# The merge's gates move into the SSM stage: one change to a fused mixer kernel on one core

## What is computed

```python
rw, ss, gates = split(h @ w_in)                      # gates: 2 * 1024 columns
ya = rwkv_branch(rw)                                 # 512 x 1024
# SSM branch, tokens in column-major order of a grid 64 wide
z, xbc, dt = split(ss)
xs, bm, cm = split(silu(conv5(xbc)))                 # 32 heads of 64, 4 groups of 8 heads
for each direction (2), group (4), chunk of 128 tokens (2 of context, then 4):
    y_inter = (c @ h) * exp(cum)                     # "old"
    y_intra = sum over the chunk of (c b) seg xdt    # "new", one product per head
    h = h * exp(total) + b^T (decay * xdt)           # "carry"
yb = rms_norm((y + d * xs) * silu(z)) * ssm_norm     # 512 x 2048
ga, gb = split(sigmoid(gates))
out = (ga * (ya @ proj_a) + gb * (yb @ proj_b)) @ w_out
```

## Time and profile before

| | |
|---|---|
| median of 3 runs | 5265.73 us (5258.98 to 5266.15) |
| profiled execution, its own time | 5250.39 us |
| its span, first to last instruction | 5248.6 us |
| SSM stage in it | 1204.7 to 1936.1 us |
| merge stage's gates and branches | 1936.1 to 2218.0 us |

### The profile page before, as it was taken

How to read it: one execution, slowest core, us unless ns; L and a number is a source line. 1 busy time by engine, 2 the same in 40 slices (tenths; PEclk the granted TensorE clock), 3 DMA queues, 4 the chain that set the end, 5 groups by cost and what they waited for, 6 DMA issues and landing times.

```text
span 5248.6 us, 82193 instructions
## 1 busy us (share of the span) xinstructions
PE 4751.9 (91%) x34820; PEld 2970.3 (57%) x34820; DVE 2125.6 (40%) x3933; ACT 1308.2 (25%) x2411; POOL 427.6 (8%) x387
## 2 busy tenths in 40 slices
PE   7889999888988869979997998989998998989999
PEld 4566666676554544454443545554777545544777
DVE  3555555553354551031112345463333245373333
ACT  2333333332222210010001133231222123231222
POOL 0111111100231230000000000010000000020000
PEclk9999999998999979989998999989999999989999
DMA  6100000001001022139996211113221211113221
GB/s 224 73 18 18 18 18 5 5 5 61 24 33 48 17 107 113 72 139 378 410 408 256 74 66 45 47 58 135 96 80 63 78 53 59 43 44 137 97 96 49
DMA packets 72775, 494.75 MB, mean 94 GB/s; under 512 B 9032, under 2 KB 9560, under 8 KB 29784
## 3 DMA queue, kind: packets, MB, share of 16 engines
q1 hardware_dynamic: 72408, 489.49, 24.1%
HBM read 468.47 MB, written 21.00 MB: 93 GB/s over the span
## 4 chain that ended last, share of the span: by engine, by line
PE 77%; DVE 9%; issue 7%; DMA 3%; ACT 2%; POOL 1%; SPq 0%; PEldq 0%; PEld 0%; POOLq 0%; DVEq 0%; ACTq 0%
PE ps L224 74%; PE ps L227 3%; DMA upper<-in_ew 2%; DVE upper L235 2%; DVE upper L243 1%; ACT upper L282 1%; DVE upper L259 1%; DVE lower L235 1%; POOL upper L3349 1%; DVE upper L251 1%; DVE lower L243 1%; ACT lower L282 0%; DVE upper L239 0%; DVE lower L251 0%; DVE lower L239 0%
## 5 line engine op out<-in xcount | busy, mean ns | idle before, releaser
L224 PE MATMUL ps<-lower 128*128 128x512 f32 (+9 forms) x6512 | 1968.3, 464 | 82.4 <-issue 25.1
L224 PEld LDWEIGHTS ps<-lower 128*128 128x128 f32 (+3 forms) x6512 | 993.5, 197 | 772.8 <-issue 596.2
L224 PE MATMUL ps<-upper 64*64 64x64 f32 (+10 forms) x14800 | 916.1, 261 | 144.8 <-DVE upper L251 48.5
L282 ACT ACTIVATE upper<-ps 128x512 f32<-128x512 f32 (+6 forms) x963 | 446.1, 484 | 2006.8 <-PE ps L224 1341.2
L224 PEld LDWEIGHTS ps<-upper 64*64 64x64 f32 (+5 forms) x14800 | 662.2, 147 | 487.7 <-issue 265.5
L224 PE MATMUL ps<-lower,upper 64*64 64x64 f32 (+6 forms) x7216 | 740.1, 320 | 54.3 <-DMA lower<-in_ada 20.0
L224 PE MATMUL ps<-rounded 128*128 128x512 f32 x3072 | 724.5, 398 | 30.7 <-DVE rounded L235 23.2
L224 PEld LDWEIGHTS ps<-rounded 128*128 128x128 f32 x3072 | 586.8, 191 | 167.6 <-ACT rounded L282 26.3
L224 PEld LDWEIGHTS ps<-lower,upper 64*64 64x64 f32 (+3 forms) x7216 | 404.9, 146 | 337.5 <-issue 280.8
L224 PE MATMUL ps<-upper,lower 128*128 128x512 f32 (+4 forms) x1584 | 512.4, 476 | 10.1 <-DVE lower L243 3.2
L282 ACT ACTIVATE upper<-upper 128x128 f32<-128x128 f32 (+11 forms) x619 | 328.3, 536 | 688.2 <-DVE upper L255 167.4
(11 more groups left out here) (81 smaller groups left out, 2189.5 us busy)
## 6 DMA issues: line engine op xcount, KB each, us to landing
lower<-in_ew SPq DMA_DIRECT2D x144, 1024.0 KB, 10.5
upper<-in_ew SPq DMA_DIRECT2D x48, 1024.0 KB, 13.5
lower<-in_b0f SPq DMA_DIRECT2D x16, 2048.0 KB, 7.6
lower<-in_b1f SPq DMA_DIRECT2D x16, 2048.0 KB, 7.5
upper<-in_ada SPq DMA_DIRECT2D x18, 1024.0 KB, 5.8
lower<-in_wrkv SPq DMA_DIRECT2D x8, 1728.0 KB, 7.6
lower<-in_b0g SPq DMA_DIRECT2D x8, 1536.0 KB, 6.3
gad<-upper SPq DMA_DIRECT2D x48, 256.0 KB, 2.0
```

Of the source, the lines that this page charges most:

```text
L224: return self.e.matmul(out, lhsT, rhs, start=start, stop=stop)
L282: self.e.activation(out, in_, func, bias=bias, scale=scale, accum_out=accum).then_inc(line.up(*event), 1)
```

## The change

The gates' 128 matmuls leave the merge stage. The projector makes them as `mgate`, t, s after its last z: 16 tiles t of four steps with two matmuls each, from column-major `b.hp`. ScalarE copies each tile out of PSUM in row-major order into one of two stages, SP stores it to a new DRAM tensor `gmd`, and the merge stage fetches it into the buffers of the sigmoid, which works in place. The weights come in tiles of 512 columns through the SSM stage's ring. The copies back to `k.hL` and the "scan" meeting go. A group is ready for the scans before its z; the projector may begin group g - 2's successor when both scans of g - 2 are through, and from its second tile on when `gated` says that z of g - 2 is used up. In `apply` each head's product is made as two, one for each half of the stationary matrix's columns (64 each), which write the two halves of the PSUM partitions. The loads of `wdt` and the first `wx` are issued by SP from the RWKV stage's list. Left out of the diff below: new scratch and line declarations, and dispatch lines.

```diff
@@ -129,7 +129,7 @@
     o["wdt"] = tiles(w[:, s + 5120:s + 5184], 64)
     g = s + 5184
     ga, gb = (w[:, g + 1024 * i:g + 1024 * i + 1024].reshape(1024, 8, 128) for i in range(2))
-    o["wg"] = tiles(np.concatenate([ga, gb], 2).reshape(1024, 2048), 256)
+    o["wg"] = tiles(np.concatenate([ga, gb], 2).reshape(1024, 2048), 512)
     o["pa"] = tiles(a["proj_a"][0], 128)
     o["pb"] = tiles(a["proj_b"][0], 128)
     o["wo"] = tiles(a["w_out"][0], 256)
...
@@ -827,6 +828,9 @@
     for name, j, *at in b.order:
         if name == "lora" and at == [1, 1] and j < 6:
             ring.load(("wrkv", j + 2), T["wrkv"][j + 2], P.pe, "lora", j + 2, 1, 1)
+        elif name == "lora" and at == [1, 1] and j == 7:
+            sp.wait_ge(P.pe, "lora", 7, 1, 1)
+            ssm_begin(k, sp)
         elif name == "ada_row" and j < 11:
             modulation(j + 1)
         elif name == "store":
@@ -1486,6 +1490,7 @@
     b.ysum = [m(512) for _ in range(2)]
     b.ysq, b.yd = m(512), m(512)
     b.yo = [m(512) for _ in range(2)]
+    b.stage = [m(512) for _ in range(2)]
     b.xd, b.xe = ([extra(512) for _ in range(2)] for _ in range(2))
     b.cbm = [extra(128) for _ in range(2)]
     b.h = [extra(512) for _ in range(2)]
...
@@ -1510,15 +1515,20 @@
 
     def projector():
         for g in range(4):
-            while g > 1 and g - 2 not in done:
+            while g > 1 and not {(g - 2, 0), (g - 2, 1)} <= scanned:
                 yield None
             for ci in range(6):
+                while g > 1 and ci and g - 2 not in gated:
+                    yield None
                 for s in range(7):
                     yield ("conv", g, ci, s)
+            ready.add(g)
             for i in range(4):
                 for s in range(2):
                     yield ("z", g, i, s)
-            ready.add(g)
+        for t in range(16):
+            for s in range(4):
+                yield ("mgate", t, s)
 
     def scanner(d):
         for g in range(4):
@@ -1538,6 +1548,8 @@
                 yield None
             for i in range(8):
                 yield ("read", g, i)
+                if i == 3:
+                    gated.add(g)
             done.add(g)
 
     proj = projector()
@@ -1555,26 +1567,37 @@
     return (k.step[d].pe, "apply", g - 1, 5) if g else None
 
 
-def ssm_sync(k, sp):
-    b, T, M, P = k.ss, k.T, k.main, k.proj
-    for e in k.end:
-        sp.wait_ge(k.end[e], "rwkv")
-    ring = Ring(sp, [k.wreg[:, 4096 * i:4096 * i + 4096] for i in range(2)])
+def ssm_begin(k, sp):
+
+    T, M, P = k.T, k.main, k.proj
+    k.ring = Ring(sp, [k.wreg[:, 4096 * i:4096 * i + 4096] for i in range(2)])
     loads = [("wdt", T["wdt"][0], M.pe, "dt")]
     for g in range(4):
         loads += [(("wx", g), T["wx"][g], P.pe, "conv", g, 3), (("wbc", g), T["wbc"][g], P.pe, "conv", g, 5),
                   (("wz", g), T["wz"][g], P.pe, "z", g, 3)]
-    loads = iter(loads)
-    ring.load(*next(loads))
-    ring.load(*next(loads))
+    loads += [(("wg", m), T["wg"][m], P.pe, "mgate", 4 * m + 3) for m in range(4)]
+    k.loads = iter(loads)
+    k.ring.load(*next(k.loads))
+    k.ring.load(*next(k.loads))
+
+
+def ssm_sync(k, sp):
+    b, T, P = k.ss, k.T, k.proj
+    for e in k.end:
+        sp.wait_ge(k.end[e], "rwkv")
     fetch(sp, b.dtb, k.row("dtb"), "dtb")
     fetch(sp, b.na, k.row("alog"), "alog")
     fetch(sp, b.dd, k.row("ssmd"), "ssmd")
     for name, *z in b.order:
-        if name == "dt" or name == "conv" and z[1:] in ([3, 3], [5, 3]) or name == "z" and z[1:] == [3, 1]:
-            load = next(loads, None)
+        if name == "mgate" and z[1] == 3:
+            t, _ = z
+            sp.wait_ge(P.act, "mgate", t)
+            sp.e.dma_start(k.gmd[t], b.stage[t % 2]).then_inc(k.kept[t % 2].up16("gate", t), 16)
+        if name == "dt" or name == "conv" and z[1:] in ([3, 3], [5, 3]) or name == "z" and z[1:] == [3, 1] or (
+                name == "mgate" and z[0] % 4 == 3 and z[1] == 3):
+            load = next(k.loads, None)
             if load:
-                ring.load(*load)
+                k.ring.load(*load)
         elif name == "read" and z[1] > 3:
             g, q = z[0], z[1] - 4
             sp.wait_ge(k.tail.dve, "out", g, q)
@@ -1630,6 +1653,20 @@
         for kk in range(4 * s, 4 * s + 4):
             last = pe.mm(at["z"], hp_token(k, kk, i), w[:, kk, :], kk == 0, kk == 7)
         if s:
+            last.then_inc(P.pe.up(*use), 1)
+            pb.give(use, P.act, *use)
+
+    def merge_gate(t, s):
+
+        use = ("mgate", t)
+        w, loaded = k.slot["wg", t // 4]
+        w = v3(w, 512)
+        if s == 0:
+            at["mgate"] = pb.take(use)
+            pe.wait_ge(loaded, "wg", t // 4)
+        for kk in (2 * s, 2 * s + 1):
+            last = pe.mm(at["mgate"], ch(w[:, kk, :], t % 4), b.hp[:, kk, :], kk == 0, kk == 7)
+        if s == 3:
             last.then_inc(P.pe.up(*use), 1)
             pb.give(use, P.act, *use)
 
@@ -1662,7 +1699,8 @@
             pe.wait_ge(team.pool, "values", g, i)
             for x in range(8):
                 v = slice(64 * x, 64 * x + 64)
-                last = pe.mm(p2[:, v], ch(b.Wt[d], x), b.xd[d][:, v], True, True)
+                for e in (slice(0, 64), slice(64, 128)):
+                    last = pe.mm(p2[e, v], ch(b.Wt[d], x)[:, e], b.xd[d][:, v], True, True)
             last.then_inc(team.pe.up("apply", g, i), 1)
             banks.give(use2, team.dve, "new", g, i)
         elif name == "carry" and i < 5:
...
@@ -1826,9 +1865,7 @@
     v.wait_ge(M.act, "yrstd")
     for i in range(4):
         v.ts(M.dve, ch(b.dg, i), c["ident"], s4[:, i:i + 1], MUL, event=("dg",) if i == 3 else ())
-    v.meet("dve", "scan")
-    for kk in (1, 4, 7):
-        v.copy(M.dve, k.hL[:, kk, :].rearrange("p (r c) -> p r c", c=64), b.hp[:, kk, :].rearrange("p (c r) -> p r c", r=8))
+    v.wait_ge(M.pe, "yrstd")
     v.copy(M.dve, k.rb.rearrange("p (r c) -> p c r", c=64), k.pair("yrstd").rearrange("p (c r) -> p c r", r=8))
     v.meet("dve", "ssm")
 
@@ -1851,9 +1888,9 @@
         n = 768 if ci < 5 else 512
         tile = 4 * g + ci if ci < 4 else (16, 20)[ci - 4] + g
         o, grp = b.o2[ci % 2], b.groups[g % 2]
-        if s == 0 and ci == 0 and g > 1:
-            a.wait_ge(tail.dve, "out", g - 2, 3)
-        elif s == 2 and ci:
+        if s == 2 and ci:
+            if ci == 1 and g > 1:
+                a.wait_ge(tail.dve, "gated", g - 2, 3)
             turn(g, ci - 1)
         elif s == 4:
             a.wait_ge(P.pe, "conv", g, ci)
@@ -1884,6 +1921,14 @@
             if s:
                 a.wait_ge(P.pe, "z", g, i)
                 a.act(P.act, b.groups[g % 2].z[:, i, :], k.pair(("z", g, i)), AF.Silu, "z", g, i)
+        elif name == "mgate":
+            t, s = z
+            if s == 3:
+                a.wait_ge(P.pe, "mgate", t)
+                if t > 1:
+                    a.wait_ge(k.kept[t % 2], "gate", t - 2)
+                a.copy(P.act, b.stage[t % 2].rearrange("p (r c) -> p c r", c=64),
+                       k.pair(("mgate", t)).rearrange("p (c r) -> p c r", r=8), "mgate", t)
         elif name in ("values", "masks"):
             g, d, i = z
             if i > 1:
...
@@ -1987,15 +2026,24 @@
     def load(name, d):
         ring.load((name, d), T[name][d], M.pe, "branch", d, 1)
 
-    load("wg", 0)
+    def gates(d):
+        if d > 1:
+            sp.wait_ge(M.dve, "mT", d - 2)
+        for br in range(2):
+            sp.e.dma_start(b.sig[br][d % 2], k.gmd[2 * d + br]).then_inc(k.line(f"gate_in{d % 2}_{br}").up16("gate", d), 16)
+
     load("pa", 0)
     for line in k.stored:
         sp.wait_ge(line)
     fetch(sp, b.yaT, k.yad.rearrange("k p t -> p k t"), "yaT")
+    for line in k.kept:
+        sp.wait_ge(line)
     load("pb", 0)
     fetch(sp, b.ybT, k.ybd.rearrange("k p t -> p k t"), "ybT")
-    for name in ("wg", "pa", "pb"):
+    gates(0)
+    for name in ("pa", "pb"):
         load(name, 1)
+    gates(1)
     fetch(sp, b.x, T["x"].rearrange("(i p) d -> p i d", p=128), "x2")
     sp.wait_ge(k.line("mrow"))
     fetch(sp, b.g1, k.mrow_bc(2048, 1024), "g1")
@@ -2004,8 +2052,9 @@
     fetch(sp, b.n2p, k.row("n2pre"), "n2p")
     fetch(sp, b.n2s, k.mrow_bc(3072, 1024), "n2s")
     for d in range(2, 8):
-        for name in ("wg", "pa", "pb"):
+        for name in ("pa", "pb"):
             load(name, d)
+        gates(d)
     for n in range(4):
         ring.load(("wo", n), T["wo"][n], M.pe, "out", 3)
 
@@ -2014,15 +2063,7 @@
     b, M = k.mg, k.main
     banks = Banks(pe, 0, 8)
     for d in range(8):
-        wg, loaded_g = k.slot["wg", d]
-        wg = v3(wg, 256)
         for br, (name, src, nk, source) in enumerate((("pa", b.yaT, 8, "yaT"), ("pb", b.ybT, 16, "ybT"))):
-            ps = banks.take(("gate", d, br))
-            pe.wait_ge(loaded_g, "wg", d)
-            for kk in range(8):
-                last = pe.mm(ps, wg[:, kk, 128 * br:128 * br + 128], k.hL[:, kk, :], kk == 0, kk == 7)
-            last.then_inc(M.pe.up("gate", d, br), 1)
```

(25 more changed lines are left out.)

## The result

The changed kernel takes **5190.5 us** (median of 4 runs, 5179.3 to 5194.6), the kernel before beside it 5262.5 us; the ratio is 0.986, with a 95% interval of 0.9841 to 0.9878. That is 72 us less. The forecast was 5187 us and 78.5 us less.

What follows compares the result with a forecast made beforehand. TensorE, busy 91% of the span, was the bound. From 1330 us, 552 us of work plus 74 lost, then 183.5 to the last branch product: 78.5 us less than before, giving 5187 us; range 5162 to 5224.

Steps and rivals of the forecast that it cites:

- The merge: Merge stage without the gates' matmuls: first issue to last branch product 183.5 us, before 281.9; 98.4 of 109.8 us gained.
- Head products: `apply` in the SSM stage: 32 half records instead of 16 whole ones gain 0.47 us per step, 15 us in all.
- The order: SSM stage: scans before z and an earlier projector remove the lone stretches; 63 us stay lost over three convolution stretches.
- The lone stretches: SSM stage, where scans or projector run alone (1484 to 1515, 1612 to 1642 us): losses of 17.5 and 14.4 become 0.
- the end: Last 30 us of the SSM stage before the merge: gate steps cover VectorE's reads; 6 us lost instead of 33.6.
- What stays over convolutions: SSM stage, scans over convolutions: `apply` waits for `weights` and low clock lose 21 us in each of three stretches, 63.
- The walk through group 1: Waits of `apply` at i = 2 to 5: about 5, 0 to 1, 3 and 2.7 us; 11.5, with low clock 19.
- The merge's first load: End of the SSM stage: the merge's first issue comes at 1956 us instead of 1936.1.
- A: Head products: halves give nothing, switches cost about 0.25 us per step; 5210 us, chance 0.08 (full load price: 5258, 0.02).
- C: SSM stage: each half-array `apply` is followed by some 7 us at 1.2 GHz, 115 us lost; 5302 us, chance 0.02.
- B: SSM stage: waits stay; last scans keep 20 of 31 us, each stretch loses 33 instead of 21; 5238 us, chance 0.11.
- A's price for the switches: Head products in `apply`: changing the tiling mode costs about 0.25 us per step, 8 us in all.

Runs made afterwards that it cites:

- early_ya: The changed kernel with the 2 MB of yaT fetched behind the last scans instead of after the SSM stage: 5185.1 us, ratio 0.9855.
- two_edits: The changed kernel with yaT fetched behind the last scans and the norm's chain put beside the last gate steps: 5179.7 us, ratio 0.9843.
- order_alone: The kernel before with only the new order of scans, z and projector; gates stay in the merge, head products whole: 5228.2 us, ratio 0.9934.
- half_adds: The changed kernel without the first half of the convolution's adds (three taps instead of five, so another computation): 5149.7 us, ratio 0.9784.
- later_apply: The changed kernel with one empty turn between `weights` and `apply` in the first three groups: 5198.9 us, ratio 0.9879.

## Why the prediction was right

**The merge.** 109.8 us out, 11.4 given back at the start; the stretch from the first issue to the last branch product was to be 183.5 us and is 183.6. Counting the bytes that stand ahead of the first operand was enough, and `early_ya`, foreseen in the same way (17.7), is a second test of it. `two_edits` (19.5) shows its limit.

**Head products.** 15 us foreseen; 16 and 17 by the medians in two settings, 12 to 17 by the stages. The estimate came from a row of the same form in another stage, against the page of the Trainium skill "TensorE: Matmul & The Clock Gate", section "LDWEIGHTS (loading the stationary operand)". By its rule a load of 64 columns takes 53 ns (an estimate from the page), and 32 of them in a row would have given nothing. The trace has 37 ns per record and pairs 58 ns apart: two loads pass in about the time that the rule gives one. The measurement decides. The Trainium skill's page "TensorEngine Tiling (Array Packing)", section "Overview", has up to twice the speed where a dimension is at most 64, as the moving one is here; 16 records of 0.11 us became 32 in 1.19, a factor of 1.5.

**The order.** The lone stretches went, as said (17.5 and 14.4 us to nothing). `order_alone` shows them at 36 us with the piece of the end. The prediction did not split the end between order and gates; the runs do.

**What stays over convolutions.** Foreseen 63 us, found 67, and here the total is better than its parts. The walk through group 1 gave `apply` waits of 5, 0 to 1, 3 and 2.7 us, 11.5 in all; the trace has 4.5, 1.9 and 1.9, 8.2 in all. The other 6.1 of the 14.3 idle us are the two waits for a PSUM bank, of which the prediction says nothing. Both kinds end with a product of VectorE that stood behind adds, and `half_adds` takes away the waits of `apply` and one of the two others; but that the sums agree is partly luck.

**Terms that were small but off.** The merge's first load stands at 1976.4, not near 1956: 10 of the 20 us come ahead of the SSM stage, 10 lie in it. The SSM stage took 1976.4 - 1214.8 = 761.6 us where 1956 - 1204.7 = 751.3 were foreseen. Four of these 10 us are the waits over the convolutions. About three lie among the gate steps, where a transpose or gate matmul waits for ScalarE or VectorE to free one of the projector's four banks (up to 1.2 us each, as in the 1.12 before the row at 1963.41). Two are a low clock at 1322 us, in the first convolution; the second profile of the kernel before has one there too, so it is no property of the change. The end took 6 as foreseen.

**Luck.** In the profiles the saving is 57.5 us: 78.5 less 10 in the SSM stage and 10 ahead of it. The working started from the first profile of before, which was a quick one, and added its distance to the median, 15.3 us. Against the second profile of the same kernel, 12.4 us lie ahead of the SSM stage and 4.3 in it, and none of that is a property of the change. The medians gave 72. So the range was right by its reasons and the 3.5 us of distance from the result are closer than the working deserved.

**Rivals.** A and C did not happen. B did not as a whole: the last scans lose a few us, not 20, and each stretch 22, not 33. But `later_apply` shows that B was near: two more projector steps in front of each `apply` bring two stretches to 32 us. A's price for the switches, 0.25 us per step, had no row behind it; the trace has about as much (0.26 behind the 32 records, 0.09 ahead). A failed on its other half: a record takes 29 ns, not half of a full one's 110. C's low clock did not follow either: the last stretch has eight `apply` steps in it and a clock of 0.99.

## What to carry to other kernels

Work that has no dependence is worth most where it fills a stage's serial end, and at its old place one must look for what it covered: here transfers of 11 us. When a wait is for an in-order engine, giving the waiting instruction more time only helps if that engine's next product isn't late as well; take work off that engine instead (41 us here, against 8 lost). When a single profile stands on each side, compare stage by stage: here the parts that nobody changed moved by more than several of the edits. Cost a new form by rows of the same form in another stage of the same trace before a rule.

## What the runs showed of the hardware

Products with 64 stationary columns each, into alternating halves of the array, take 37 ns per fp32 record at the full clock, against 108 to 112 ns for a record with 128 columns. Their records start in pairs, 58 ns from pair to pair, which is 29 ns each; the way back to the full array (0.26 us per 32) is inside the 37, about 0.09 us of the way in is not. Between two profiles of the same program the SSM stage started 12 us apart; 10 of these stood before the RWKV stage's first store, behind 200 us with a granted clock of 0.91 in one and 0.83 in the other. That is more than several of the effects measured here.
